# A half unit, a down unit, the second tile of x, one wait and two transfers put elsewhere in the order of a decoder-layer kernel

## The reference

```
h = rms_norm(x, g_attn)
qa, ka, va, fa, qb, kb, vb, ga, gb = split(h @ w_in)      # 2048 x 10248
o_a = fox_attention(qk_norm(qa), qk_norm(ka), va, log_sigmoid(fa + b_forget))
o_b = dilated_attention(qk_norm(qb), qk_norm(kb), vb, slopes)
x = x + (sigmoid(ga) * (o_a @ w_br_fox) + sigmoid(gb) * (o_b @ w_br_dil)) @ w_out
u = rms_norm(x, g_ffn) @ w_up                             # 2048 x 11264
conv = sum(w_conv[t] * shifted(u, t) for t in range(3)) + b_conv
gate, val = split(conv)
x = x + (silu(gate) * val) @ w_down                       # 5632 x 2048
```

## Time and profile before

| | us |
|---|---|
| time, median of 3 runs | 1339.59 (1339.37 to 1339.69) |
| the profiled execution, its time | 1339.67 |
| the profiled execution, its span | 1337.7 |
| PE busy | 1329.5 (99% of the span) |
| DVE busy | 1121.9 (84%) |
| ACT busy | 940.9 (70%) |
| POOL busy | 156.2 (12%) |

### The profile page before, as it was taken

How to read it: one execution, slowest core, us unless ns; L and a number is a source line. 1 busy time by engine, 2 the same in 40 slices (tenths; PEclk the granted TensorE clock), 3 DMA queues, 4 the chain that set the end, 5 groups by cost and what they waited for, 6 DMA issues and landing times.

```text
span 1337.7 us, 16446 instructions
## 1 busy us (share of the span) xinstructions
PE 1329.5 (99%) x6055; PEld 1101.2 (82%) x6055; DVE 1121.9 (84%) x1333; ACT 940.9 (70%) x1180; POOL 156.2 (12%) x175
## 2 busy tenths in 40 slices
PE   9999999999999999999999999999999999999999
PEld 7888888888888888888878888888888888888887
DVE  6768787888878876657789898999999999999995
ACT  6666666566666654446777778888888888888872
POOL 0121212021011000001010101111111102020200
PEclk9999999999999999999999999999999999999999
DMA  9878685758888654667879688999989899999952
GB/s 331 289 184 266 138 257 122 242 154 233 229 215 230 209 176 170 214 225 225 271 174 326 156 304 172 313 220 287 243 251 267 230 288 214 304 205 311 206 197 91
DMA packets 118175, 305.73 MB, mean 229 GB/s; under 512 B 11848, under 2 KB 13136, under 8 KB 117584
## 3 DMA queue, kind: packets, MB, share of 16 engines
q1 hardware_dynamic: 92288, 234.57, 50.4%
q0 software_dynamic: 21728, 66.07, 27.7%
q10 hardware_dynamic: 4080, 4.05, 0.9%
HBM read 302.55 MB, written 2.11 MB: 228 GB/s over the span
## 4 chain that ended last, share of the span: by engine, by line
PE 97%; DMA 1%; ACT 1%; DVE 0%; issue 0%; SPq 0%; ACTq 0%; DVEq 0%
PE acc L740 13%; PE acc L744 13%; PE acc L742 13%; PE acc L778 9%; PE acc L782 9%; PE acc L780 9%; PE acc L959 4%; PE acc L963 4%; PE acc L961 4%; PE acc L936 3%; PE acc L934 3%; PE acc L938 3%; PE acc L1071 1%; PE acc L764 1%; PE acc L760 1%; PE acc L762 1%
## 5 line engine op out<-in xcount | busy, mean ns | idle before, releaser
L1752 DVE TENSOR_TENSOR w_lo<-raw,w_hi 128x1024 fp32r<-128x1024 f32 x234 | 283.8, 1221 | 89.4 <-ACT w_hi L1239 88.3
L1239 ACT ACTIVATE w_hi<-raw 128x1024 fp32r<-128x1024 f32 x234 | 244.9, 1054 | 113.4 <-PE acc L744 77.5
L740 PE MATMUL acc<-w_hi,actA 128*128 128x512 f32 x664 | 261.6, 394 | 0.5 <-DVE w_lo L1752 0.4
L744 PE MATMUL acc<-w_hi,actA 128*128 128x512 f32 x664 | 258.9, 390 | 0.0
L742 PE MATMUL acc<-w_lo,actA 128*128 128x512 f32 x664 | 258.4, 389 | 0.0
L1239 ACT ACTIVATE w_hi<-raw_y 128x1024 fp32r<-128x1024 f32 x144 | 149.7, 1058 | 71.6 <-PE acc L744 21.6
L1752 DVE TENSOR_TENSOR w_lo<-raw_y,w_hi 128x1024 fp32r<-128x1024 f32 x144 | 173.2, 1220 | 24.1 <-ACT w_hi L1239 23.0
L1752 DVE TENSOR_TENSOR w_lo<-raw_x,w_hi 128x1024 fp32r<-128x1024 f32 x108 | 130.1, 1221 | 42.4 <-ACT w_hi L1239 42.3
L744 PEld LDWEIGHTS acc<-w_hi,actA 128*128 128x128 f32 x664 | 124.6, 188 | 26.5
L740 PEld LDWEIGHTS acc<-w_hi,actA 128*128 128x128 f32 x664 | 124.7, 188 | 26.2 <-issue 1.5
L742 PEld LDWEIGHTS acc<-w_lo,actA 128*128 128x128 f32 x664 | 124.8, 188 | 25.1
(11 more groups left out here) (297 smaller groups left out, 2597.7 us busy)
## 6 DMA issues: line engine op xcount, KB each, us to landing
raw<-w_in SPq DMA_DIRECT2D x102, 512.0 KB, 4.7
raw<-w_down SPq DMA_DIRECT2D x59, 512.0 KB, 5.7
raw_x<-w_up SPq DMA_DIRECT2D x44, 512.0 KB, 5.0
raw_y<-w_up POOLq DMA_DIRECT2D x34, 512.0 KB, 7.2
raw_x<-w_in SPq DMA_DIRECT2D x28, 512.0 KB, 4.1
raw<-w_out SPq DMA_DIRECT2D x28, 512.0 KB, 4.4
odd<-w_up SPq DMA_DIRECT2D x27, 512.0 KB, 5.2
work<-w_up SPq DMA_DIRECT2D x24, 512.0 KB, 5.4
```

The costliest lines, as they stand in the source:

```text
L740: nc.tensor.matmul(o, lhsT=a_h, rhs=w_hi[:, s, k, :], start=first and k == 0, stop=False, skip_group_check=onto_seed)
L744: mm = nc.tensor.matmul(o, lhsT=a_l, rhs=w_hi[:, s, k, :], start=False, stop=last and k == KU - 1, skip_group_check=onto_seed)
L1239: nc.scalar.activation(w_hi[:, n % RING, :, :], src.rearrange("p (k n) -> p k n", k=KU), ACT.Copy).then_inc(hi_done, 1)
L1752: nc.vector.tensor_tensor(w_lo[:, n % RING, :, :], src.rearrange("p (k n) -> p k n", k=KU), w_hi[:, n % RING, :, :].bitcast(f32), ALU.subt ...
```

## The change

Five things stand elsewhere in the order; no instruction is added or taken out, and none computes anything else.

1. Half a plain unit: the first row half of U(1,1,0) is done ahead of P5 of block 1 in place of behind it (`EARLY_ROW`).
2. A down unit: in block 10, D(9,2) comes after P4 in place of before it. DVE's `older_tap(10, 0, 0)`, which stood behind D(9,2)'s split, stands behind P4's first, so it keeps its place.
3. The second tile of x: ACT and DVE split both tiles of x ahead of the second weight tile.
4. A wait: ACT and DVE wait for `ident_in` behind unit 13's split in place of ahead of unit 6's.
5. The two transfers of x by rows stand two weight tiles later in SP's queue each.

```diff
--- before.py
+++ after.py
@@ -36,6 +36,7 @@
...
 WHOLE = 3
+EARLY_ROW = (1, 1, 0)
 
...
@@ -200,7 +201,8 @@
...
             units += product("P3") + down(4) + product("P1") + product("P7") + down(5) + product("P6") + down(6)
-            units += down(7) + product("P5") + down(0) + down(1) + product("P2") + down(2) + product("P4") + down(3)
+            units += down(7) + product("P5") + down(0) + down(1) + product("P2")
+            units += product("P4") + down(2) if i == BLOCKS - 1 else down(2) + product("P4") + down(3)
             continue
...
@@ -628,10 +630,11 @@
...
                         load(1, 1, 1024)
-            sp.dma_start(xr[:, 0, :], x_rows[:, 0, :]).then_inc(x_in[0], 16)
             for u in range(2, UPR):
...
                 if u == 3:
+                    sp.dma_start(xr[:, 0, :], x_rows[:, 0, :]).then_inc(x_in[0], 16)
+                elif u == 5:
                     sp.dma_start(xr[:, 1, :], x_rows[:, 1, :]).then_inc(x_in[1], 16)
...
@@ -747,11 +750,12 @@
...
 
-            def plain_unit(n, act, kts, o0, o1, u0_wait):
+            def plain_unit(n, act, kts, o0, o1, u0_wait, rows=(0, 1)):
 
...
                 s = n % RING
-                for r, o in enumerate((o0, o1)):
+                for r in rows:
+                    o = (o0, o1)[r]
                     if r == 1 and u0_wait:
...
@@ -763,7 +767,8 @@
...
                                               stop=kt == KT - 1, skip_group_check=True)
-                mm.then_inc(used, 1)
+                if 1 in rows:
+                    mm.then_inc(used, 1)
 
...
@@ -1117,13 +1122,13 @@
...
 
-            def plain_up(n, i, side, j):
+            def plain_up(n, i, side, j, rows=(0, 1)):
                 if i == 0 and side == 1 and j % 2 == 0:
...
                 act = actA if kt < 3 * CT else actB
-                plain_unit(n, act, (kt, kt + 1), o0[:, :], o1[:, :], i + 1 if side and j == 0 else 0)
+                plain_unit(n, act, (kt, kt + 1), o0[:, :], o1[:, :], i + 1 if side and j == 0 else 0, rows)
 
...
@@ -1164,7 +1169,7 @@
...
                     _, i, side, j = unit
-                    plain_up(n, i, side, j)
+                    plain_up(n, i, side, j, (1,) if (i, side, j) == EARLY_ROW else (0, 1))
                     continue
...
@@ -1173,6 +1178,8 @@
...
                 _, i, name, q = unit
+                if unit == ("S", EARLY_ROW[0], "P5", 0):
+                    plain_up(AT[("U",) + EARLY_ROW], *EARLY_ROW, (0,))
                 product(n, i, name, q)
...
@@ -1337,15 +1344,15 @@
...
 
-            for kt in range(KU):
+            def first_high(kt):
                 act.wait_ge((first_tile, w_loaded[0])[kt], 16)
...
                     .then_inc(tile_high, 1)
-                if kt == 0:
-                    act.wait_ge(gains_in, 16)
-                    act.wait_ge(xt_in[0], 16)
-                nc.scalar.activation(actA[:, kt, 0:SEQ], xt[:, kt, :], ACT.Copy,
-                                     scale=smalls_sb[:, S_GATT + kt:S_GATT + kt + 1]).then_inc(h_hi, 1)
+
+            first_high(0)
+            act.wait_ge(gains_in, 16)
+            scaled_high(0)
+            first_high(1)
             act.wait_ge(second_tile, 16)
...
@@ -1361,7 +1368,6 @@
...
 
-            act.wait_ge(ident_in, 32)
             turned = {11: (0, 0), 12: (0, 1), 20: (1, 0), 22: (1, 1)}
...
@@ -1382,6 +1388,8 @@
...
                 high(slot + RING)
+                if slot == UPR - 1:
+                    act.wait_ge(ident_in, 32)
                 if slot < 2:
...
@@ -1889,13 +1897,15 @@
...
 
-            dve.wait_ge(gains_in, 16)
-            for kt in range(KU):
+            def first_low(kt):
                 dve.wait_ge(tile_high, kt + 1)
...
                                         w_hi[:, 0, kt, :].bitcast(f32), ALU.subtract).then_inc(tile_split, 1)
-                dve.wait_ge(h_hi, kt + 1)
-                scaled_low((actA[:, kt, SEQ:2 * SEQ], actA[:, kt, 0:SEQ]), kt, xt[:, kt, :], S_GATT, h_lo)
+
+            dve.wait_ge(gains_in, 16)
+            first_low(0)
+            scaled_lows(0)
+            first_low(1)
             dve.wait_ge(tile_high, KU + 1)
...
@@ -1972,9 +1982,10 @@
...
 
-            dve.wait_ge(ident_in, 32)
             for slot, (R, u) in enumerate(HEAD_UNITS):
                 low(slot + RING)
+                if slot == UPR - 1:
+                    dve.wait_ge(ident_in, 32)
                 if slot < 2:
...
@@ -2255,7 +2266,7 @@
...
                         last_low("P5")
-                    elif u == 2 and WHOLE <= i + 1 < BLOCKS:
+                    elif u == 2 and WHOLE <= i + 1 < BLOCKS - 1:
                         older_tap(i + 1, 0, 0)
...
@@ -2304,7 +2315,7 @@
...
                     older_tap(i, 0, 1)
-                elif unit == ("S", FULL, "P4", QU):
+                elif unit in (("S", FULL, "P4", QU), ("S", BLOCKS - 1, "P4", 0)):
                     older_tap(i, 0, 0)
...
```

## The result

The changed kernel takes 1341.87 us (median of 21 runs, 1339.97 to 1344.04), the kernel before 1340.04 on the same chip (21 runs, 1339.37 to 1341.27). The ratio is 1.0014, with a 95% interval of 1.0008 to 1.0020: 1.83 us slower, where +0.71 was predicted. Each run also lists its mean granted clock, and the runs of the changed kernel fall into two groups by it: seven at 1.000 (median 1340.51) and fourteen at 0.999 or 0.997 (median 1342.19). This split is what the study is about.

The account below looks back on a forecast made before the run. PE was taken to bound the kernel, busy 1329.5 of 1337.7 us. Terms -0.20 - 0.63 + 0 + 2.57 - 1.03 = +0.71 on the profiled 1339.67 gave 1340.4, median 0.08 lower: 1340.3 us, range 1338.6 to 1341.9.

Parts of the forecast that it names:

- the third rival: Block 1: the longer wait, 3 us, lets PE's clock fall, costing 2.1 us, time 1342.3; chance 7%.
- the likeliest case: Whole kernel: the summed terms hold, +0.71, predicted 1340.3 us, own range 1339.6 to 1341.3; chance 64%.
- Its price: Cost of a clock fall in block 1: 2.1 us, taken from the warm-up's nine matmuls at 0.46 each.
- The half unit: Block 1: one wait that cost 1.5 becomes two costing 3.1 and 1.1, +2.57 us, bounds +2.2 and +2.9.
- The down unit: End of block 10: DVE's L2199 comes one split earlier, PE's wait at L1071 goes, -1.03 us, bounds -0.7 and -1.1.
- this rival: End of block 10 wins nothing, or a wait on `a_lo` takes its place: +1.0, 1341.3 us; chance 7%.
- The wait for `ident_in`: Head, unit 6: without ACT's wait the split is early and PE's whole wait goes, -0.63 us, bounds -0.63 and 0.
- the second tile: Head, unit 0: second half starts 0.40 earlier, unit 2 is then late, leaving -0.20 us, bounds 0 and -0.40.
- The transfers of x's rows: Head: later transfers of x still land in time for PE's transposes, cost 0; up to 0.83 back if not.
- The second rival: Head: x's second half lands after 36.8, the 0.83 us won are lost in part or whole, 1341.1; chance 15%.
- Signs asked for: Changed profile: listed start times and waits at units 0, 2, 6, transposes, block 1, block 10, plus conditions that refute the prediction.
- The other sign: Head: a wait showing up between 24 and 80 us would make the prediction wrong.

Follow-up runs that it names:

- e1: Kernel before with only the half unit of U(1,1,0) moved ahead of P5: 1345.01 us (5 runs), +5.36 to before.
- e11: Changed kernel with 3 matmuls of unused result ahead of the half unit, leaving 2.1 us idle: 1341.65 us, +1.58 to before.
- e10: Kernel before with only the half unit moved ahead of P5, measured once more: 1343.48 us (7 runs), +3.4 to before.
- e9: The changed kernel measured again, nothing altered: 1341.86 us (11 runs), +1.79 to before.
- e2: Changed kernel with 12 matmuls of unused result filling the wait ahead of the half unit: 1340.42 us, +0.77 to before.
- e5: Changed kernel with 6 matmuls of unused result ahead of the half unit, filling half of the wait: 1340.36 us, +0.65 to before.
- e6: Kernel before with only the half unit moved and its wait filled with 12 unused matmuls: 1342.10 us, +2.39 to before.
- e3: Changed kernel without the half unit's move, all other edits kept: 1338.11 us, -1.54 to before.
- e4: Kernel before with only the down unit of block 10 moved: 1338.96 us, -0.69 to before.
- e12: Changed kernel without the half unit's move and with x's second tile back in its old place: 1337.71 us, -2.36 to before.
- e8: Changed kernel without the half unit's move and with both transfers of x's rows at their old places: 1337.90 us, -1.81 to before.
- e7: Changed kernel without the half unit's move, ACT copying P6's sum ahead of U(1,1,1)'s split: 1337.95 us, -1.76 to before.

## Why the prediction was wrong, point by point

**The step that failed** is the third rival's chance: "It decides if the longer idle time is enough for a fall. Chance 7%." The longer idle time is enough in 31 of 44 runs. In the sum of +0.71 the clock has no term; it stood outside the likeliest case, at 7%. The mechanism, its place and its sign were named. What argued against it were waits of at most 1.3 us, which say nothing about one of 3: the table has 1 of 66 at 0.8 to 1.4 us, and 5 of 11 at 2.1. With the fall in most runs, the median is at the level of the runs with a fall. The measured 1341.87 lies just inside the stated range, which ends at 1341.9, but by luck: that range left the clock's case out, and was wide for waits that did not come. The likeliest case's own upper end was also set too low for its terms: 1339.59 + 2.2 is 1341.8 and not 1341.3.

**Its price** was 2.1, from the nine matmuls of the warm-up. Measured: 1.4 (e1), 1.6 (e11: ten starts in 3.98, 701.81 to 705.79, less 2.27 and 0.14), 1.6 (e10: 4.22 in block 1 less 2.6) and 2.8 (e9) in the profiles, 1.68 between the medians of the two groups of the changed kernel. So 2.1 was a little high for most falls and too low for the one in e9.

The Trainium skill (TensorE: Matmul & The Clock Gate, "HAM oscillation — how this bites in real kernels") was right in kind: waits between bursts of matmuls bring the lower clock back, and the rise is paid again. The trace of e9 agrees, with 0.50 granted from 703 to 707 us.

**The half unit**, +2.57: right. Block 1 costs +2.62 in the changed kernel, +2.59, +2.63 and +2.60 in e2, e5 and e6, where the clock holds, and e6 measures +2.39 in time. Both waits came out as worked out, 2.76 and 0.87.

**The down unit**, -1.03: right against before's profile, -0.99 to -1.06 in all ten profiles that have it, and -0.69 (-2.3 to +0.1 by the interval) in time. Before's wait of 0.9 is again one execution's: e1, e6 and e10, which lack the edit, wait 0.7 there and stand at -0.2, and against them it wins 0.85. Of this rival, that the end of block 10 wins nothing, no profile shows anything.

**The wait for `ident_in`**, -0.63, and **the second tile**, -0.20: their sum, -0.83, fits. It is -0.85 by the medians of e3 and e4. In the nine profiles with edits in the head it lies between -0.12 and -1.07, with a median of -0.81. The parts are another matter, and the start of unit 2 on PE parts them. In the eight profiles with the second tile moved PE starts unit 2 between 11.89 and 12.44 (median 12.16), in the six without between 11.70 and 12.40 (median 12.11). Nothing of the 0.20 shows, and neither does it in e12: the lower bound, 0, was the value. In before's profile PE came 0.28 later than its split asked for, and none of the five other profiles with the old order has so long a wait at the second tile; I read one execution's as the kernel's.

From unit 2 on, up to the second matmul of unit 6, all nine profiles with the wait for `ident_in` moved win 0.51 to 0.56 against before, among them e12, without the second tile's move, and e8, without that of x's rows. So it is this edit's, though no kernel has it alone. Of the profiles that keep the wait there, e1 and e10 stand like before, within 0.05, while e4 and e6 lose another 0.64 and 0.49, with 0.9 us idle at unit 6 in place of 0.4. The edit is worth 0.5 to 1.2 by the execution that one compares with.

**The transfers of x's rows**, 0: right as far as e8 tells (-1.81 against -1.54 for e3, each uncertain by more than the difference). The cover of the transposes held, at 47.86 without idle time; with the transfers at their old place e4 waits 0.53 there, before and e1 don't. The second rival, that x comes late to the transposes and the head gives back what it won, is seen in no profile with the move. A wait at 61 us does take back 0.4 in the first profile and 0.3 in e8, and nothing in e2, e3, e5, e9, e11 and e12, but that one is for a weight tile.

So the waits sum to +0.71 as predicted, and the runs in which the clock held measure it: +0.47 by the median of seven, +0.28 and +0.53 in two of e9. To this comes the clock in 23 of 32 runs.

Signs asked for: the second half of unit 0 at 7.8 (7.56), a new wait at unit 2 of 0.1 (0.41 idle, at the same time as before), none at unit 6 (true), transposes at 47.6 (47.86), 2.7 to 3.0 and 0.9 in block 1 (2.76 and 0.87), none at the end of block 10 (true; the matmuls run on at 0.23). "If PE's matmuls after it start more than 0.4 us apart" was the sign of the failure, and it is what e1, e9, e10 and e11 show. The other sign, a wait between 24 and 80 us, came too, in the first profile: 0.37 idle at 61.24; e9, the same kernel, doesn't have it.

What stays open: why the clock falls in one execution and not in the next of the same kernel, and why the stretch at the lower clock has 7 starts in one profile and 14 in another. A longer wait ahead of P5 without the half unit was not tried.

Of the versions here e3, e7, e8 and e12 beat both kernels, by 1.5 to 2.4 us against before; they can't be told from each other. All leave the half unit out.

## What to carry to other kernels

Price a wait of TensorE in two parts, the time it stands still and what it may do to the clock, and take the second part seriously as soon as the wait is longer than any the trace has shown to be harmless. A run's mean clock of 0.999 in place of 1.000 is a finding: over 1340 us it is a fall of 1.6 us (e10, e11), and the one of 2.8 us reads 0.997 (e9), which a page in 40 slices can't show. If a wait can't be avoided, matmuls that compute nothing take back what the clock would cost (1.1 us here), but moving the work so that the wait stays short is better by another 2.3 (e2 to e3). And a wait seen in one execution's head is that execution's: have a second profile before you price it.

## What the runs showed of the hardware that I had not expected

- The clock went down once behind a wait of only 1.13 us and the eight matmuls of 8 columns that followed (e1 at 62 us: 0.43 from start to start for the matmuls from 63.85 on). In e10 a wait of 1.4 at the same place left it up.
- It can go down after the wait is over: in e11 the first matmul behind a wait of 2.07 still took the full-speed 0.50, the third 0.63.
- How long the slow starts go on differs: 3.1 us in e1 (705.30 to 708.43), 3.4 in e11 (702.39 to 705.79), and 6.1 in e9 (702.21 to 708.34).
- The first matmul behind a wait ran 0.34 to the next start in block 1 (703.58 to 703.92), and the matmuls behind it 0.23; six took 1.49 in place of 1.36.
